# Rotary embeddings: the partner rows fetched by VectorE's lane shuffle instead of by a TensorE permutation, and each tile turned directly behind its own products

## What is computed

```python
def apply_axial_rope(x, cos, sin):            # first model, dr = 32 or 64
    q = x.shape[-1] // 4
    xr1, xr2, xc1, xc2 = jnp.split(x, 4, axis=-1)
    return jnp.concatenate([xr1*cr - xr2*sr, xr1*sr + xr2*cr,
                            xc1*cc - xc2*sc, xc1*sc + xc2*cc], axis=-1)

def first_layer(...):                          # l = 0, 1
    z = h @ w_in                               # c_q, c_kv, k_r, dq, dk, dv, ga, gb
    q = rms_norm(c_q, g_q) @ w_uq              # qn, qr
    kv = rms_norm(c_kv, g_kv) @ w_ukv          # kn, va
    qr, kr, q1, q2, k1, k2 = rotated (latent tokens only)
    o_a = softmax(qn.kn + qr.kr) @ va          # attention A, 8 heads
    o_b = (softmax(q1.k1) - lam*softmax(q2.k2)) @ vb   # attention B, 4 heads
    x = x + gate*merge(o_a, o_b); x = x + gate*conv_ffn(x)

def partial_rope(x, cos, sin):                 # second model, first 16 of 64 dims
    x1, x2 = x[..., :8], x[..., 8:16]
    rot = jnp.concatenate([x1*c - x2*s, x2*c + x1*s], axis=-1)
    return jnp.concatenate([rot, x[..., 16:]], axis=-1)

def second_layer(...):                         # l = 0, 1
    qa, ka, va, qi, ki, wi, qb, kb, vb, rb, gl, uc = split(h @ w_in)
    qa, ka, qi, ki = partial_rope of each
    # top-128 keys of each query by an index score from qi, ki, wi; attention over those
    o_a = attend(qa, ka, va, top_k(score(qi, ki, wi)))
    o_b = gated_linear_attention(qb, kb, vb, gate(gl))
    o_c = multiscale_pool(uc)
    x = x + concat(o_a, o_b, o_c) @ w_out; x = x + conv_glu_ffn(x)
```

## Time and profile before

| | |
|---|---|
| time, median of 3 runs | 3504.97 us (3501.03 to 3505.96) |
| span of the profiled execution | 3503.3 us |
| PE busy | 3411.7 us, 97% |
| DVE busy | 2092.1 us, 60% |
| ACT busy | 1318.7 us, 38% |
| POOL busy | 122.4 us, 3% |
| granted TensorE clock | 0.9 or more of full speed in all 40 slices |

### The profile page before, as it was taken

How to read it: one execution, slowest core, us unless ns; L and a number is a source line. 1 busy time by engine, 2 the same in 40 slices (tenths; PEclk the granted TensorE clock), 3 DMA queues, 4 the chain that set the end, 5 groups by cost and what they waited for, 6 DMA issues and landing times.

```text
span 3503.3 us, 45971 instructions
## 1 busy us (share of the span) xinstructions
PE 3411.7 (97%) x18212; PEld 2726.2 (78%) x18212; DVE 2092.1 (60%) x3304; ACT 1318.7 (38%) x2084; POOL 122.4 (3%) x70
## 2 busy tenths in 40 slices
PE   7999999999999999999999999998999999899998
PEld 5866788888888887767777888776888877688886
DVE  5856653465576655445547664696666449756643
ACT  4454443333213324544434333445322234632222
POOL 0000000000000000000000000150000006000000
PEclk9999999999999999999999999999999999999999
DMA  6411111111362231101122233220232332122332
GB/s 260 147 43 43 49 72 55 61 55 60 111 225 90 100 106 59 38 25 43 61 92 84 94 96 105 91 89 20 91 93 93 105 103 79 43 71 92 96 97 95
DMA packets 79221, 300.56 MB, mean 86 GB/s; under 512 B 8784, under 2 KB 8912, under 8 KB 77904
## 3 DMA queue, kind: packets, MB, share of 16 engines
q1 hardware_dynamic: 77760, 291.47, 25.4%
q10 hardware_dynamic: 1296, 6.82, 0.5%
HBM read 296.16 MB, written 2.10 MB: 85 GB/s over the span
## 4 chain that ended last, share of the span: by engine, by line
PE 89%; DVE 7%; ACT 2%; issue 1%; DMA 0%; POOL 0%; SPq 0%; DVEq 0%; ACTq 0%
PE ps L756 25%; PE ps L758 24%; PE ps L757 24%; PE ps L1075 2%; PE ps L1117 1%; PE ps L1141 1%; PE ps L1155 1%; PE ps L1162 1%; PE ps L1132 1%; DVE work L2945 1%; PE ps L1018 1%; DVE top L2944 1%; PE ps L774 1%; PE ps L1020 1%; PE ps L1019 1%; PE ps L811 1%
## 5 line engine op out<-in xcount | busy, mean ns | idle before, releaser
L2201 DVE TENSOR_TENSOR split<-raw,split 128x1024 fp32r<-128x1024 f32 x406 | 497.2, 1225 | 802.3 <-ACT split L1595 801.7
L1595 ACT ACTIVATE split<-raw 128x1024 fp32r<-128x1024 f32 x436 | 460.2, 1056 | 757.6 <-PE ps L758 685.2
L756 PE MATMUL ps<-h,split 128*128 128x512 f32 x1320 | 528.3, 400 | 0.0
L758 PE MATMUL ps<-h,split 128*128 128x512 f32 x1320 | 520.8, 395 | 0.0
L757 PE MATMUL ps<-h,split 128*128 128x512 f32 x1320 | 520.7, 394 | 0.0
L756 PEld LDWEIGHTS ps<-h,split 128*128 128x128 f32 x1320 | 248.7, 188 | 64.9 <-issue 7.4
L756 PE MATMUL ps<-h_hl,split 128*128 128x512 f32 (+1 forms) x752 | 285.0, 379 | 12.0 <-DVE h_hl L2281 8.9
L757 PEld LDWEIGHTS ps<-h,split 128*128 128x128 f32 x1320 | 248.7, 188 | 59.8 <-issue 3.4
L758 PEld LDWEIGHTS ps<-h,split 128*128 128x128 f32 x1320 | 248.6, 188 | 58.0
L758 PE MATMUL ps<-h_hl,split 128*128 128x512 f32 (+1 forms) x752 | 266.7, 355 | 0.0
L757 PE MATMUL ps<-h_hl,split 128*128 128x512 f32 (+1 forms) x752 | 266.3, 354 | 0.0
(11 more groups left out here) (441 smaller groups left out, 6361.6 us busy)
## 6 DMA issues: line engine op xcount, KB each, us to landing
raw<-wstream SPq DMA_DIRECT2D x442, 512.0 KB, 3.5
ada_t<-ada_w SPq DMA_DIRECT2D x80, 512.0 KB, 4.5
first_w<-ada_first SPq DMA_DIRECT2D x4, 2048.0 KB, 24.9
x<-x_in SPq DMA_DIRECT2D x1, 3072.0 KB, 12.9
x<-x_in ACTq DMA_DIRECT2D x1, 3072.0 KB, 10.9
ada_c<-c_in SPq DMA_DIRECT2D x2, 1024.0 KB, 5.2
out<-x SPq DMA_DIRECT2D x8, 256.0 KB, 2.2
par<-params SPq DMA_DIRECT2D x1, 1345.0 KB, 6.1
```

The costliest lines, as they stand in the source:

```text
L756: nc.tensor.matmul(o, wh, a[0], start=first, stop=False)
L758: return nc.tensor.matmul(o, wl, a[0], start=False, stop=last)
L1595: nc.scalar.activation(split_of(n)[:, 0, :], raw[:, n % RAW_SLOTS, :], copy).then_inc(hi_split, 1)
L2201: nc.vector.tensor_tensor(split_of(n)[:, 1, :], raw[:, n % RAW_SLOTS, :], split_of(n)[:, 0, :].bitcast(F32), ALU.subtract).then_inc(split_ ...
```

## The change

The permutation matrices, the matmuls and ACT's copies go. DVE fetches the partner rows itself with STREAM_SHUFFLE, which permutes the rows within each group of 32, from the tile into `rot`, and then runs the same three operations. The sign that the matrix held moves into the tables: on the host for the first model, by one extra factor (`turn_sign`) in the second. The parameter tile `par`, 128 rows of fp32, becomes 383 columns narrower. The waits for a free `rot` buffer move from ACT to DVE, and DVE waits for ACT's take of the tile itself (`landed`). In the lists a rotation stands directly behind its own tile's products, and in `key_fills` it no longer counts as a piece with a weight, so the dk products spread over the steps a little differently.

```diff
+PARTNERS_A = [i ^ (ROPE_A // 4) for i in range(32)]
+PARTNERS_B = [i ^ (DH_B // 4) for i in range(32)]
+PARTNERS_2 = [i ^ (ROT // 2) if i < ROT else i for i in range(32)]
 def roped(tiles):
-    events, pending = [], None
+    events = []
     for name, groups, rope in tiles:
         events += [("gemm", name, g) for g in groups]
-        if pending is not None:
-            events.append(("rot", pending, None))
-        pending = name if rope else None
-    if pending is not None:
-        events.append(("rot", pending, None))
+        if rope:
+            events.append(("rot", name, None))
     return events
...
-    events += [("norm", "squares", None)] + tile_of(("dq", 0), G) + [("rot", ("kr", 0), None)] + tile_of(("dq", 1), G)
-    events += [("norm", "sums", None), ("rot", ("dq", 0), None)] + tile_of(("dq", 2), G)
-    events += [("norm", "spread", None), ("rot", ("dq", 1), None)] + tile_of(("dq", 3), G) + [("rot", ("dq", 2), None)]
+    turned = lambda m: tile_of(("dq", m), G) + [("rot", ("dq", m), None)]
+    events += [("norm", "squares", None), ("rot", ("kr", 0), None)] + turned(0) + tile_of(("dq", 1), G)
+    events += [("norm", "sums", None), ("rot", ("dq", 1), None)] + tile_of(("dq", 2), G)
+    events += [("norm", "spread", None), ("rot", ("dq", 2), None)] + turned(3)
...
-    after = {("qr", 0): ("dq", 3), ("qr", 1): ("qr", 0), ("qn", 0): ("qr", 1)}
     for name in Q_TILES:
         events += tile_of(name, G)
-        if name in after:
-            events.append(("rot", after[name], None))
+        if name[0] == "qr":
+            events.append(("rot", name, None))
...
         if kind == "rot":
-            pieces.append((2.5, (kind, name, g, DC - 1)))
+            pieces.append((0.0, (kind, name, g, DC - 1)))
...
-        units += tile_of(("dk", m), BOTH)
-        if m:
-            units.insert(len(units) - 1, ("rot", ("dk", m - 1), None))
-    return laid_out(units + [("rot", ("dk", H_B - 1), None)], l, True)
+        units += tile_of(("dk", m), BOTH) + [("rot", ("dk", m), None)]
+    return laid_out(units, l, True)
...
 IN2_INDEX = (plain(("qi", 0), ("qi", 1), "kgw") + [("rot", ("qi", 0), None), ("rot", ("qi", 1), None)]
-             + plain(("uc", 0)) + [("rot", "ki", None), ("turn", "wi", None)])
+             + [("rot", "ki", None)] + plain(("uc", 0)) + [("turn", "wi", None)])
...
-            def rotate(perm, src, after, bank=None):
-                pe.wait_ge(acc_taken, after)
-                o = open_acc(SEQ, bank)
-                nc.tensor.matmul(o, col(perm, 0, P), src, start=True, stop=True).then_inc(acc_ready, 1)
...
-                    bring(rot[l][rot_place(l, name, k)][:, :], o)
...
-            def rope(dst, rotated, cos, sin):
+            def rope(dst, rotated, cos, sin, partners):
+                v(nc.vector.stream_shuffle(rotated, dst, partners))
                 v(nc.vector.tensor_tensor(rotated, rotated, sin, ALU.mult))
                 v(nc.vector.tensor_tensor(dst, dst, cos, ALU.mult))
                 return nc.vector.tensor_tensor(dst, dst, rotated, ALU.add)
...
-                nc.vector.tensor_tensor(sin2[:, :], sin_t[:, :], rs_in[:, :], ALU.mult).then_inc(tab_made, 1)
+                nc.vector.scalar_tensor_tensor(sin2[:, :], sin_t[:, :], col("turn_sign"), rs_in[:, :], ALU.mult, ALU.mult)\
+                    .then_inc(tab_made, 1)
```

More of the change, by code:

```diff
@@ L891, in two_products, with project @@
                                 mm.then_inc(slab_used if g == groups[-1] else part_ready, 1)
-            def project(events, weight, act, perm, src, fresh=False, norm_step=None, layer=None, at=None,
-                        beside=()):
+            def project(events, weight, act, fresh=False, norm_step=None, layer=None, at=None, beside=()):
                 at, w = dict(at or {}), None
@@ L976, in mla @@
                 events = lora_events(l)
-                project(events, weight, act, perm, src, fresh=True, norm_step=step, beside=beside)
-                rots.add(4)
-                dq3 = res.now(back=1)
+                project(events, weight, act, fresh=True, norm_step=step, beside=beside)
+                rots.add(5)
                 wait_hl(5)
-                project_after(up_events(l), weight, act, perm, src, {("dq", 3): dq3})
-                rots.add(3)
+                project_after(up_events(l), weight, act)
+                rots.add(2)
                 w = open_slab()
@@ L995, in project_after @@
                         t0, K, opens, closes, last = weight(name)
-                        if opens and name not in at:
+                        if opens and name not in opened:
                             w = open_slab()
+                        opened.add(name)
                         gemm(w, t0, K, act(name), g, closes and g == last)
-                        at[name] = res.n
-                    else:
-                        rotate(perm(name), src(name), at[name])
             def own_tokens(l, groups):
@@ L1098, in fill @@
                         if k == 0:
-                            if name not in at:
+                            if name not in opened:
                                 at["w"] = open_slab()
+                            opened.add(name)
                             at["o"] = open_acc(g[1], NORM_BANK)
-                            at[name] = res.n
                         mm = product(at["o"], at["w"], k, cols(h_hl)(k, g), k == 0, k == DC - 1)
@@ L2465, in turn @@
                 if kind == "kr":
-                    dst, tab = kr[l][:, CTX:TOK], ropeA[l]
+                    dst, tab, partners = kr[l][:, CTX:TOK], ropeA[l], PARTNERS_A
                 elif kind == "qr":
-                    dst, tab = qr[l][:, m, SEQS[l] - SEQ:], ropeA[l]
+                    dst, tab, partners = qr[l][:, m, SEQS[l] - SEQ:], ropeA[l], PARTNERS_A
                 elif kind == "dq":
-                    dst, tab = dq[l][:, m, SEQS[l] - SEQ:], ropeB[l]
+                    dst, tab, partners = dq[l][:, m, SEQS[l] - SEQ:], ropeB[l], PARTNERS_B
                 else:
-                    dst, tab = dk[l][:, m, CTX:TOK], ropeB[l]
-                dve.wait_ge(acc_taken, res.now())
-                rope(dst, rot[l][rot_place(l, name, k)][:, :], tab[:, 0, :], tab[:, 1, :]).then_inc(rot_done, 1)
+                    dst, tab, partners = dk[l][:, m, CTX:TOK], ropeB[l], PARTNERS_B
+                dve.wait_ge(acc_taken, landed[name])
+                if l == 0 and kind == "dk":
+                    dve.wait_ge(rot_done, k)
+                elif k >= 2:
+                    dve.wait_ge(rot_done, k - 1)
+                rope(dst, rot[l][rot_place(l, name, k)][:, :], tab[:, 0, :], tab[:, 1, :], partners).then_inc(rot_done, 1)
+            landed = {}
             def settle(l, kind, name, g):
-                res.add()
                 if kind == "rot":
                     turn(l, name)
-                elif closes_slab(name, g):
+                    return
+                res.add()
+                landed[name] = res.n
+                if closes_slab(name, g):
                     split_low()
@@ L2868, in results @@
                             continue
-                        res.add()
+                        if kind != "rot":
+                            res.add()
+                            landed[name] = res.n
                         if kind == "gemm":
```

57 lines of the change are left out of this document (12 added, 45 removed).

## The result

The changed kernel takes 3511.96 us (median of 16 runs, 3507.3 to 3515.36) against 3504.95 (16 runs, 3500.7 to 3508.9): 1.0019 times as long, 95% interval 1.0013 to 1.0026, or 6.7 us more (4.6 to 9.1). The prediction was 3502.9, or 2.1 us less; the measured time lies in its range, 3486 to 3514, on the other side of no change.

A forecast was written before the change was run, and what follows sets the result against it. PE bounds the kernel nearly everywhere, but DVE is fullest where the rotations lie. The terms -0.5 - 0.35 - 2.05 + 3.3 - 3.7 + 1.2 sum to -2.1 us, so 3502.9 us, range 3486 to 3514.

The forecast's parts named there:

- term 6: Second model: a gain upstream against a moved wait downstream, net +0.6 us per layer, +1.2 for two.
- Rival A: Whole kernel: PE's work is all that counts, so removing the rotations gives 3463 us; chance 0.06.
- The shuffle, 0.80 us: Each rope on DVE: one shuffle adds 0.80 us, bounds 0.41 and 1.37; 36 of 44 count.
- Term 6, upstream of D: Second model, up to D, the end of the search: D comes 2.5 us earlier, bounds 1 and 5.
- Term 6, downstream: Second model after the search: qa3's split moves behind ACT's exponentials; gated attention's second half at D + 46.9, against D + 43.8.
- term 3: Inputs of attention, layer 1: two rotations fewer ahead of PE's norm wait, little from the other five; -2.05 us.
- term 5: Attention A, layer 1: no dot products, ropes fit gaps ahead of the scaling; -3.7 us.
- term 2: Inputs of attention, layer 0: DVE is full, its chain starts earlier but its ropes grow longer; -0.35 us.
- Term 4: Attention A, layer 0: two dk ropes delay the scaling, PE idles over 4 us each; +3.3, bounds -5 and +6.
- Term 1: Start: the parameter tile loses 196 KB of loading ahead of the first weights; -0.5 us.
- Rival C: DVE stretches: the shuffle is dear, 1.3 us instead of 0.80, giving 3521 us; chance 0.14.
- Rival B: Layer 0's attention and second model: ropes fall into DVE's gaps, the placed waits don't bind; 3491 us, chance 0.18.

The follow-up runs named there:

- c_second: Kernel before, with the whole change in the second model's two layers only, direct order: 3511.97 us, ratio 1.0025.
- x_none: Kernel before without rotation matmuls, copies or any shuffle (partner rows left out of the result), old order: 3487.10 us, ratio 0.9954.
- x_noshuf: Changed kernel without its shuffles (partner rows left out of the result), direct order kept: 3492.74 us, ratio 0.9963.
- r_index: Kernel before, shuffle for dk, layer 1's kr, dq, qr (3494.20 us with these alone), plus qi and ki of both second-model layers: 3500.72 us.
- r_roped: Kernel before, shuffle for dk, layer 1's kr, dq, qr (3494.20 us with these alone), plus qa and ka of both second-model layers: 3501.25 us.
- x_pool: Changed kernel, POOL's first split of each second-model layer held back until the three index ropes are done: 3514.25 us, ratio 1.0029.
- c_first: Kernel before, with the whole change in the first model's two layers only, direct order: 3505.71 us, ratio 1.0008.
- e1_late: Changed kernel with every list in the old order, rotations behind the next tile's products: 3510.66 us, ratio 1.0017 to the kernel before.
- e3_busy: Changed kernel with matmuls of unused result put on PE ahead of its new waits: 3509.74 us, ratio 1.0014 to the kernel before.

## Why the prediction was wrong

The kernel was forecast within noise and slightly faster; it is slower by 6.7 us. The step that failed is term 6, the second model: +1.2 us was forecast, and c_second measured +8.8 (5.6 to 11.9). Step by step:

- *What bounds.* Right: DVE, not PE, fills the stretches with rotations. Rival A (3463) needed PE to be alone; even x_none, without a permutation on any engine, is at 3487.
- *The shuffle, 0.80 us.* It measured 0.73, and the 0.41 end was rightly given little weight. The Trainium skill's figure ("VectorE: DVE Perf Modes", section "The perf-mode tier table"), divided by four, gave an estimate of 600 ns, below the measured 735. That about 36 of 44 shuffles bind was nearly right for the second shuffle (28.6 us against 27), but the first costs 19.7 (give or take 5) where 36 x 0.80 = 28.8 was counted. Less these 28.8, the forecast of -2.1 leaves -30.9 for all the rest; x_noshuf measured -13. So two sizes were too large, by some 9 us the shuffles' cost and by some 18 what the removal brings, and that half of the second error was covered by the first is luck.
- *Term 6, upstream of D.* "I take D 2.5 earlier", by 2.6 us less on PE and a stretch of ki's rope gone. Counted from the stage's first split on ACT (2236.55 before, 2234.47 in the changed kernel), D comes 2.2 us earlier in the first layer and 0.5 later in the second. And 1.8 of it is not the work that the term counts: the last step of the search, `far`, ran beside POOL before, in 2.25 us, and takes 0.43 now, in both layers. The stretch of a rope was not gone either: in the first layer it falls on the second qi rope instead (2.10 us), in the second on that and on ki's (2.12 and 2.86). The prediction had PE's logits waiting for nothing; they wait 2.40 and 4.67 us.
- *Term 6, downstream.* The moved split was followed rightly: POOL works on it from D + 5.4, and PE begins qa3 at D + 8.3, as forecast (it idles 3.35 and 3.85 us, not some 5). But "DVE starts its ropes at D + 8.9 as before" failed: POOL's two splits now fall on the two operations ahead of the ropes (2.46 and 2.58 us, of which before one was stretched, 2.51, and one took 0.41), and the ropes start at D + 11.0 in both layers. From the stage's start DVE so reaches qa0's rope when it did before in the first layer and 2.6 us later in the second, and PE reaches the second half of the gated attention 1.6 and 4.2 us later than before, where 0.6 was forecast for each. In the second layer it then runs at half clock, from 3013.5 to 3027.0.
- r_index and r_roped put 7.4 and 8.4 us on the two parts of the stage by the ratios, in the old order, together more than c_second's 8.8. x_pool shows that a single collision can't be taken out of the sum: with the ropes freed of it the time did not fall. How much of the 8.8 each wait makes stays open.
- *Terms 2 to 5, -2.8 us.* In the traces these stages sum to -4.0 (changed) and -4.6 (c_first): term 3 was right, term 5 gave 1.1 more than counted, term 2 was off by 1.3 the other way. But c_first's median is +2.8 (0 to 6.0). The surplus doesn't lie in these stages in its trace, and its cause stays open. In layer 0 dq1's rope, which was let "go ahead of the norm" free of charge, stands ahead of the norm's scaling on DVE, and PE idles 4.80 us at 140.83, and 3.08 instead of 1.37 in layer 1. That rope is not what makes them, at least in layer 1: in e1_late it stands behind the scaling, and PE still waits 3.24 and 3.09 us there. So it can answer for at most 1.6 us of the wait in layer 0.
- *Term 4.* The mechanism was right: PE idle 3.27 us ahead of the transposes, twice, with a fall of the clock behind each; the prediction had "over 4 us". The stage cost 1.5 us, not 3.3.
- *Term 1, -0.5.* Not to be seen: at 107 us the changed kernel is 0.02 us ahead of the kernel before, and c_first, whose parameter tile did not shrink, 0.4.
- *Clock falls.* The prediction counted four at 1.6 us at most as a rival; the trace has 58 us more at half clock. e3_busy shows that the falls behind the new waits are worth little by themselves. Falls in general are not free (next paragraph).
- *Rival C* ended on the right side for another reason; its dear shuffle does not exist. Rival B's condition, that ropes find gaps in layer 0's attention, is true only in the old order.

**Read with care.** The granted clock falls in different places in different executions, and this moves single spans by several us. Up to the second model the kernel before and c_second have the same instructions (c_second's parameter tile is one column wider). Their traces (windows of both, before first):

```profile
527.00:537.30 10.30, 10.30 (x46) 9.91 (x46) 2.82 (x10) 5.40 (x7) 0.00 (x0) 0.50 0.19 52
...
527.00:537.30 10.30, 10.30 (x64) 9.12 (x64) 2.83 (x10) 5.45 (x7) 0.00 (x0) 1.00 0.17 52
```

PE is busy throughout in both, and at half clock it got through 46 matmuls instead of 64; behind this stretch c_second is 4.6 us further ahead. So a fall of 10.3 us where PE binds cost about half its length. Likewise the second model's stages hold 23.9 us less at half clock in c_second's trace than in the changed kernel's, with the same lists, and take some 4 us less. And among the executions of one kernel the slow ones have the lower mean clock: of the 27 executions of the kernel before that stand beside e1_late, 3500.25 us went with 0.993 and 3512.4 with 0.989. The changed kernel's median clock is 0.983, that kernel's 0.991. How much of the 6.7 us that makes was not separated; e3_busy raised the median clock to 0.988 and brought some 2 us, its own added matmuls included.

So the spans that put 0.7 us of the loss into the second model's first layer and 6.8 into the second are one execution's. c_second's profiled span is only 3502.7 while its median is 3511.97, and its executions reach from 3503.98 to 3516.55. That the 8.8 us of the second model and the 2.8 of the first exceed the 6.7 of both is within their intervals.

## What to carry to other kernels

Moving work off the busiest engine pays only where the engine that takes it has a gap at that place: ask each stretch, not the mean share (60% for DVE here, and 95 to 97% in two of the stretches that mattered). The same exchange gave -11 us for the eight dk rotations, and +6.7 for all 44. "Directly behind its own products" is not early or late by itself: put the moved operation behind what another engine waits for, as dk's rope behind the scaling, which was worth 9.5 us by the ratios, 5.3 of them in the two attention stages of the traces. In the inputs of layer 1 the direct order was the better one, by 3.9 us of a trace. And a lighter engine arrives earlier at the next wait, so a term for what it saves needs the other side's arrival beside it.

## What the runs showed of the hardware

A 128x512 fp32 STREAM_SHUFFLE took 0.73 us and its LOAD_MASK_SELECT 0.01, the next operation starting 0.75 us behind the shuffle's start (231.53 to 232.28 in the changed kernel). Operations of a rope, with two SBUF inputs, took 2.12 and 2.86 us beside POOL's split instead of 0.69, and a TENSOR_SCALAR with one fp32 input 2.58 instead of 0.41. Two of the 44 shuffles ran wholly beside a POOL split, at 2248.88 and 2881.65, and took 0.75 and 0.73 us, as elsewhere. The second of them:

```profile
2881.65 0.73 DVE L2409 STREAM_SHUFFLE rot<-qi 128x512 f32<-128x512 f32 x1
```

PE's granted clock fell to half behind or within each of the eight waits listed for the changed kernel (2.40 us and more), and also behind the small matmuls of the gated attention, from 3013.5 to 3027.0, without a long wait. Matmuls with unused results in the waits (e3_busy) cut the time at half clock from 105.8 to 58.0 us. Where PE was busy throughout, 10.3 us at half clock put it 4.6 us behind an execution without that fall.
